# Block 1 of a retention and sliding-window encoder: weight chunks go ahead of raw pieces and stores in SyncE's queue, and one low part moves among the additions

## The chip, the cores and the metric

The kernel runs on one core of a Trainium2 chip. The metric is the device time of one execution in microseconds (us); lower is better. The kernel before takes 2468.24 us, the median of 3 runs (2468.12 to 2469.08).

## The reference

Two layers over x of 2048 tokens by 1024 channels, all float32:

```
h = x
h = h + retention(rmsnorm(h)) # q, k, v, gate = h @ w_in (1024 x 6144); 4 heads, chunkwise recurrence,
                              # o normalised per head, y = o * silu(gate), y @ w_out (2048 x 1024)
kb, vb = banded keys and values of rmsnorm(h) @ w_kv
h = h + swa(rmsnorm(h))       # q, gate = h @ w_in (1024 x 2048); window of 128 tokens with sinks,
                              # y = o * silu(gate), y @ w_out
return rmsnorm(h)
```

## The kernel before

**Blocks, heads and chunks.** The tokens are worked in 4 blocks of 512, each all the way through both layers. A block has four retention heads and then a "post" part with the second layer. The weights of a head come in 8 chunks, c0 to c7 (q, k, v in two halves, gate in two halves, output in two halves); the post part has 14. Each float32 operand is split into a high and a low part that TensorE can multiply, and each product is three matmuls (`three`, L674 to L676: high by high, high by low, low by high). A chunk is then 2048 KB of high and low parts. It needs 48 matmuls of 128x512 in every part of a head spoken of here. There are two chunk buffers, `whl0` and `whl1`, for even and odd chunks.

**Where the split chunks come from.** Block 0 loads raw weights, splits them (GpSimd the high part, VectorE the low part), uses them, and stores them to `split_w` in HBM (`store_chunk`, L419). Block 1 loads them from there (`load_split`, L438, in heads; L536 in the post part). `load_split` of chunk c waits on `w_used` until chunk c-2, which lay in the same buffer, has been used by TensorE. TensorE in its turn waits for a chunk's landing on `w_ready` (`w_wait`).

**The combining work of block 1.** Blocks 2 and 3 use other weights, sums of quarters of the raw ones. Block 1 makes these on the side, in each head six pieces, j = 0 to 5:

1. SyncE loads raw weights into `raw`, buffer j % 2, in two DMAs of 512 KB (`load_piece`, L463).
2. GpSimd forms the four sums (L619) and then the high part into `stage`, a part of `ff` (L625). There is one stage only, so the high part of piece j waits until both stores of piece j-1 have landed (`comb_stored`).
3. VectorE forms the low part of each piece but the fifth (`comb_less_hi`, L1857); of that one GpSimd does it itself. VectorE works in program order, so an instruction behind L1857 waits while L1857 waits for GpSimd's high part.
4. SyncE stores both parts in two DMAs of 1024 KB (`store_piece`, L473), after waiting for the low part.

The low parts of pieces 0, 1, 2, 3 stand at fixed places in VectorE's program: piece 0 between the two rotations (after q's low part, before the rotation of k, L1869), piece 1 behind k's low part, piece 2 just before the low parts of v (L1560), piece 3 behind the last state update, piece 5 behind the eight additions to the residual (L1978). TensorE starts the state updates and outputs of a head when its chunk c3 (second half of v) is done and two of the four low parts of v are there (`v_lo`).

**SyncE's queue.** SyncE issues all of these DMAs, in the order in which `combining_head` is written, and waits in that order. In a head h > 0 the order is: c0, c1, store of piece 5 of the head before, raw piece 1, c2, store 0, raw 2, c3, store 1, raw 3, c4, store 2, raw 4, c5, store 3, raw 5, c6, c7, store 4, raw piece 0 of the next head. In head 0 the raw pieces 0 and 1 stand first, behind a wait for the landing of all stores of block 0 (L433). ScalarE issues four stores of the finished rows of block 0 (L1276, 512 KB each) in head 0 of block 1.

Of the kernel before, what the change touches and what calls it, by code (L numbers as in the profile page):

```python
# [54 lines left out]
CHUNK = 2048  # L55
# [7 lines left out]
BLOCK_CHUNKS = HEADS * HEAD_CHUNKS + POST_CHUNKS  # L63
# [45 lines left out]
def build(nc, x, x_t, stream, rope_a, rope_b, mask, ident, ret_cols, gains, sinks, fnorm, out):  # L109
    with ExitStack() as ctx:  # L110
# [3 lines left out]
        def count(name, **kw):  # L114
            return Count(ctx.enter_context(nc.semaphore(name)), **kw)
# [118 lines left out]
        w_stored = [count(f"w_stored{i}", head=4, post=7, unit=16) for i in range(2)]  # L234
# [169 lines left out]
        def _(sp):  # L404
# [11 lines left out]
            def store_chunk(n):  # L416

                sp.wait_ge(w_ready[n % 2].sem, 16 * (n // 2 + 1))
                sp.dma_start(split_w[n * P:(n + 1) * P, :, 0:width(n)],  # L419
                             whl[n % 2][:, :, 0:width(n)].bitcast(F32)).then_inc(w_stored[n % 2].sem, 16)  # L420
# [8 lines left out]
                if n >= 1:  # L429
                    store_chunk(n - 1)  # L430
            store_chunk(BLOCK_CHUNKS - 1)
            for i in range(2):
                sp.wait_ge(w_stored[i].sem, 16 * (BLOCK_CHUNKS // 2))  # L433

            def load_split(at, c, src, width):

                sp.wait_ge(w_used.sem, at(w_used, c - 1))
                sp.dma_start(whl[c % 2][:, :, 0:width].bitcast(F32), src).then_inc(w_ready[c % 2].sem, 16)  # L438

            def split_rows(h, c):  # L440
                n = h * HEAD_CHUNKS + c
                return split_w[n * P:(n + 1) * P, :, :]
# [4 lines left out]
            def combining_head(b, h, last_store=None):  # L447
                at = Place("head", b, h)

                def load_piece(h, j):  # L450

                    if j >= 2:
                        sp.wait_ge(comb_lo.sem, Place("head", b, h)(comb_lo, j - 1))
                    elif h > 0:
                        sp.wait_ge(comb_lo.sem, Place("head", b, h - 1)(comb_lo, PIECES - 1 + j))
                    for i in range(2):
                        if j < 2:
                            n = h * HEAD_CHUNKS + 6 + i
                            src = stream[n * P:(n + 1) * P, :].rearrange("p (a i n) -> p a i n", a=2, i=2)[:, :, j, :]
                        else:  # L460
                            n = h * HEAD_CHUNKS + 2 + 2 * i
                            src = stream[n * P:(n + 2) * P, (j - 2) * 512:(j - 1) * 512].rearrange("(c p) n -> p c n", p=P)
                        sp.dma_start(raw[j % 2][:, i * HALF:(i + 1) * HALF].rearrange("p (a n) -> p a n", a=2), src).then_inc(comb_raw[j % 2].sem, 16)  # L463

                def store_piece(j):

                    sp.wait_ge(comb_lo.sem, at(comb_lo, j + 1))
                    for i in range(2):
                        if j < 2:
                            dst = comb_w[4 * h * P:4 * (h + 1) * P, i, j * 512:(j + 1) * 512]  # L470
                        else:
                            dst = vg_w[4 * h * P:4 * (h + 1) * P, i, (j - 2) * 512:(j - 1) * 512]
                        sp.dma_start(dst.rearrange("(q p) n -> p q n", p=P),  # L473
                                     stage[:, i, :].rearrange("p (q n) -> p q n", q=4)).then_inc(comb_stored.sem, 16)

                if h == 0:
                    load_piece(0, 0)
                    load_piece(0, 1)
                for c in range(3):
                    load_split(at, c, split_rows(h, c), CHUNK)  # L480
                    if c == 1 and h > 0:
                        last_store()
                        load_piece(h, 1)
                store_piece(0)
                load_piece(h, 2)
                load_split(at, 3, split_rows(h, 3), CHUNK)
                store_piece(1)
                load_piece(h, 3)
                load_split(at, 4, split_rows(h, 4), CHUNK)
                store_piece(2)  # L490
                load_piece(h, 4)
                load_split(at, 5, split_rows(h, 5), CHUNK)
                store_piece(3)
                load_piece(h, 5)
                for c in (6, 7):
                    load_split(at, c, split_rows(h, c), CHUNK)
                store_piece(4)
                if h < HEADS - 1:
                    load_piece(h + 1, 0)
                return lambda: store_piece(5)  # L500
# [40 lines left out]
            last_store = None  # L541
            for h in range(HEADS):
                last_store = combining_head(1, h, last_store)
# [1009 lines left out]
        def _(dve):  # L1553
# [56 lines left out]
            at = Place("start")  # L1610
# [24 lines left out]
            def one_block(b, first, last, combine=False):  # L1635
# [214 lines left out]
                def one_head(h, seam=False):  # L1850
                    at = Place("head", b, h)
                    n0 = h * HEAD_CHUNKS if first else None

                    def comb_less_hi(j):

                        dve.wait_ge(comb_hi.sem, at(comb_hi, j + 1))
                        dve.tensor_tensor(stage[:, 1, :].bitcast(F32R), raw[j % 2], stage[:, 0, :], ALU.subtract).then_inc(comb_lo.sem, 1)  # L1857
# [114 lines left out]
                    def add_to_h(n, t):  # L1972
                        if t < 3:
                            dve.wait_ge(out_mm.sem, at(out_mm, 3 * n + t + 1))
                        else:
                            dve.wait_ge(w_used.sem, at(w_used, 7 + n))
                        cols = hres[:, t, n * 512:(n + 1) * 512]
                        dve.tensor_tensor(cols, cols, ps[:, 4 * n + t, :], ALU.add).then_inc(h_add.sem, 2)  # L1978
# [22 lines left out]
                        split_chunk(n0 + 8)  # L2001
                    for t in range(TT):
                        add_to_h(1, t)
                    if combine:
                        comb_less_hi(5)

                if first:
                    for h in range(HEADS):
                        one_head(h)
                elif b >= FAST:  # L2010
                    for h in range(HEADS):
                        fast_head(h)
                else:
                    one_head(0, True)
                    with dve.Fori(1, HEADS) as h:
                        one_head(h)
                n0 = HEADS * HEAD_CHUNKS

                at = Place("post", b)
# [286 lines left out]
```

## Time and profile before

| | |
|---|---|
| median of 3 runs | 2468.24 us |
| the profiled execution, its own time | 2471.62 us |
| span of its trace | 2469.8 us |
| granted TensorE clock, mean | 0.994 |
| TensorE busy | 2410.3 us, 98% |
| VectorE, ScalarE, GpSimd busy | 58%, 27%, 17% |
| heads of block 1, as times in the span | 642 to 1101 us |
| DMA share of the 16 engines in 1000 to 1050 us | 1.00, at 383 GB/s |
| chunk load L438, median from issue to landing | 11.8 us (7.9 to 19.0) |
| stores L473, median to landing | 7.6 us (4.2 to 14.7) |
| raw pieces L463, median to landing | 9.5 us (4.2 to 15.4) |

Times of rows are microseconds from the start of the span. TensorE is busy for nearly the whole span, so what counts is each stretch in which it waits, and the stretches at half of its clock that come after longer waits. In the heads of block 1 every other engine has idle time, and the DMA engines are near their limit.

### The profile page before, as it was taken

The page shows a single profiled execution, that of the slowest core. Times are in us where ns is not written, and L with a number is a line of the kernel's source. Part 1 is how long each engine was busy: PE and PEld are TensorE (multiplying, and loading weights), DVE is VectorE, ACT ScalarE, POOL GpSimd, SP SyncE. Part 2 cuts the span into 40 slices and gives each one's busy share as a digit, 9 for nine tenths or more (in the row PEclk, how much of TensorE's full clock was granted, in tenths as well). Part 3 has the DMA queues.
Part 4 walks back from the last instruction along what each step waited for, and adds up shares of the span by engine and source line. Part 5 has one row for each costly group of instructions (what it writes and reads, how often), then busy time and mean ns, then how long its engine had stood idle before and what let it go on. Part 6 is the DMA issues. An engine that isn't in the chain of part 4 may idle for free.

```text
span 2469.8 us, 28619 instructions
## 1 busy us (share of the span) xinstructions
PE 2410.3 (98%) x11264; PEld 1978.4 (80%) x11264; DVE 1431.9 (58%) x2010; ACT 666.7 (27%) x1450; POOL 414.3 (17%) x310
## 2 busy tenths in 40 slices
PE   7999999999989999999999999999999999999998
PEld 6888888877768787878888888888888887888886
DVE  6555655677545545553758564655567745657374
ACT  2212312235121211121442231223352212313143
POOL 2111111221244545430001000000001100001000
PEclk9999999999999999999999999999999999999999
DMA  8667565645698898975259878775447977787433
GB/s 349 269 230 289 208 255 228 232 183 210 247 351 329 316 350 306 358 253 189 101 207 324 275 251 290 246 258 211 149 163 234 334 263 272 255 277 251 171 103 145
DMA packets 126393, 613.25 MB, mean 248 GB/s; under 512 B 8544, under 2 KB 9312, under 8 KB 104288
## 3 DMA queue, kind: packets, MB, share of 16 engines
q1 hardware_dynamic: 117424, 575.94, 64.5%
q10 hardware_dynamic: 8880, 36.18, 3.9%
q8 instruction: 49, 0.80, 0.1%
q14 instruction: 40, 0.33, 0.0%
HBM read 459.00 MB, written 153.09 MB: 248 GB/s over the span
## 4 chain that ended last, share of the span: by engine, by line
PE 83%; DVE 9%; DMA 4%; issue 2%; ACT 1%; POOL 1%; SPq 1%; DVEq 0%; ACTq 0%; POOLq 0%
PE ps L674 26%; PE ps L676 26%; PE ps L675 26%; DMA whl<-split_w 2%; PE ps L1127 2%; DVE ff L1857 1%; DMA comb_w<-ff 1%; DVE ff L2077 1%; PE ps L1137 1%; DVE ff L1965 1%; DVE fr L1556 1%; PE ps L935 1%; PE ps L822 1%; ACT ff L1424 1%; DVE mx L2117 1%
## 5 line engine op out<-in xcount | busy, mean ns | idle before, releaser
L674 PE MATMUL ps<-whl,xhi 128*128 128x512 f32 (+1 forms) x1088 | 418.4, 385 | 11.3 <-DMA whl<-split_w 6.9
L676 PE MATMUL ps<-whl,xlo 128*128 128x512 f32 (+1 forms) x1088 | 412.8, 379 | 0.0
L675 PE MATMUL ps<-whl,xhi 128*128 128x512 f32 (+1 forms) x1088 | 411.6, 378 | 0.0
L674 PE MATMUL ps<-xhi,whl 128*128 128x512 f32 x768 | 305.4, 398 | 21.6 <-DVE xlo L1560 16.2
L676 PE MATMUL ps<-xhi,whl 128*128 128x512 f32 x768 | 301.4, 392 | 0.0
L675 PE MATMUL ps<-xlo,whl 128*128 128x512 f32 x768 | 300.9, 392 | 0.0
L674 PE MATMUL ps<-whl,fr 128*128 128x512 f32 x704 | 282.1, 401 | 2.4 <-DVE whl L1598 2.1
L676 PE MATMUL ps<-whl,fr 128*128 128x512 f32 x704 | 278.8, 396 | 0.0
L675 PE MATMUL ps<-whl,fr 128*128 128x512 f32 x704 | 278.4, 395 | 0.0
L674 PEld LDWEIGHTS ps<-whl,xhi 128*128 128x128 f32 x1088 | 205.7, 189 | 50.4 <-DMA whl<-split_w 7.4
L676 PEld LDWEIGHTS ps<-whl,xlo 128*128 128x128 f32 x1088 | 205.5, 189 | 38.9
L675 PEld LDWEIGHTS ps<-whl,xhi 128*128 128x128 f32 x1088 | 205.8, 189 | 36.4
L674 PEld LDWEIGHTS ps<-xhi,whl 128*128 128x128 f32 x768 | 145.5, 189 | 51.5 <-issue 17.8
L674 PE MATMUL ps<-fr 128*128 128x512 f32 (+1 forms) x464 | 169.6, 365 | 5.3 <-DVE fr L1560 4.6
L676 PEld LDWEIGHTS ps<-xhi,whl 128*128 128x128 f32 x768 | 145.3, 189 | 31.3
L675 PEld LDWEIGHTS ps<-xlo,whl 128*128 128x128 f32 x768 | 145.7, 190 | 29.3
L675 PE MATMUL ps<-fr 128*128 128x512 f32 (+1 forms) x464 | 167.6, 361 | 0.0
L676 PE MATMUL ps<-fr 128*128 128x512 f32 (+1 forms) x464 | 167.4, 361 | 0.0
L674 PEld LDWEIGHTS ps<-whl,fr 128*128 128x128 f32 x704 | 132.4, 188 | 34.8 <-DVE whl L1598 2.3
L676 PEld LDWEIGHTS ps<-whl,fr 128*128 128x128 f32 x704 | 132.4, 188 | 32.0
L675 PEld LDWEIGHTS ps<-whl,fr 128*128 128x128 f32 x704 | 132.5, 188 | 30.4
L619 POOL TENSOR_TENSOR raw<-raw 128x512 f32<-128x512 f32 x96 | 143.9, 1499 | 16.9 <-DMA raw<-in_stream 11.2
(199 smaller groups left out, 3703.3 us busy)
## 6 DMA issues: line engine op xcount, KB each, us to landing
whl<-split_w SPq DMA_DIRECT2D x68, 2048.0 KB, 8.6
whl<-split_w SPq DMA_DIRECT2D x110, 1024.0 KB, 6.8
split_w<-whl SPq DMA_DIRECT2D x44, 2048.0 KB, 7.2
whl<-vg_w SPq DMA_DIRECT2D x64, 1024.0 KB, 6.7
raw<-in_stream SPq DMA_DIRECT2D x44, 1024.0 KB, 9.4
vg_w<-ff SPq DMA_DIRECT2D x32, 1024.0 KB, 8.3
raw<-in_stream SPq DMA_DIRECT2D x50, 512.0 KB, 9.5
whl<-comb_w SPq DMA_DIRECT2D x24, 1024.0 KB, 6.4
```

The costliest lines, as they stand in the source:

```text
L619: pool.tensor_tensor(dst, plus, minus, ALU.subtract).then_inc(comb_sum.sem, 1)
L674: pe.matmul(dst, lhs[0], rhs[0], start=start, stop=False)
L675: pe.matmul(dst, lhs[0], rhs[1], start=False, stop=False)
L676: return pe.matmul(dst, lhs[1], rhs[0], start=False, stop=stop)
L822: tr = pe.transpose(ps[:, 4 + t, e * P:(e + 1) * P], on[:, t, e * P:(e + 1) * P], idt[:, :])
L935: tr = pe.transpose(ps[:, 4 + t, e * P:(e + 1) * P], on[:, t, e * P:(e + 1) * P], idt[:, :])
L1127: mm = pe.matmul(ps[:, 4 + s % 2, r * 256:(r + 1) * 256], qt[:, i, n, 2 * r:2 * r + 2, :].rearrange("p f c -> p (f c)"), kwin[:, :, n // 2 ...
L1137: tr = pe.transpose(ps[:, 6, j * P:(j + 1) * P], probs[:, s % 2, j, :], idt[:, :])
L1424: act.activation(on[:, t, :], ps[:, 4 + t, :], ACT.Identity, scale=oscale[:, t:t + 1], bias=obias[:, t:t + 1]).then_inc(o_norm.sem, 1)
L1556: return dve.tensor_tensor(dst, src, hi.bitcast(F32), ALU.subtract).then_inc(c.sem, 1)
L1857: dve.tensor_tensor(stage[:, 1, :].bitcast(F32R), raw[j % 2], stage[:, 0, :], ALU.subtract).then_inc(comb_lo.sem, 1)
L1965: dve.tensor_tensor(on[:, t, :], on[:, t, :], sg[:, t, :], ALU.mult).then_inc(y_done.sem, 1)
```

## The change

Block 1's part of SyncE's program is put in another order, and one VectorE instruction moves.

- The wait for all stores of block 0 goes. The first chunk waits only for the stores from its own buffer, and is issued ahead of raw pieces 0 and 1; the second chunk waits for the stores from the other buffer.
- In every head c3 is issued before store 0 (and before raw piece 2). c4 stays behind store 1 and goes ahead of raw piece 3; c5 and c6 likewise go ahead of raw pieces 4 and 5. c7 comes behind raw piece 5.
- The low part of piece 5 goes behind the sixth addition to the residual instead of the eighth.

```
-            for i in range(2):
-                sp.wait_ge(w_stored[i].sem, 16 * (BLOCK_CHUNKS // 2))
...
                 if h == 0:
+                    sp.wait_ge(w_stored[0].sem, 16 * (BLOCK_CHUNKS // 2))
+                load_split(at, 0, split_rows(h, 0), CHUNK)
+                if h == 0:
                     load_piece(0, 0)
                     load_piece(0, 1)
-                for c in range(3):
+                    sp.wait_ge(w_stored[1].sem, 16 * (BLOCK_CHUNKS // 2))
+                load_split(at, 1, split_rows(h, 1), CHUNK)
+                if h > 0:
+                    last_store()
+                    load_piece(h, 1)
+                for c in (2, 3):
                     load_split(at, c, split_rows(h, c), CHUNK)
-                    if c == 1 and h > 0:
-                        last_store()
-                        load_piece(h, 1)
                 store_piece(0)
                 load_piece(h, 2)
-                load_split(at, 3, split_rows(h, 3), CHUNK)
                 store_piece(1)
+                load_split(at, 4, split_rows(h, 4), CHUNK)
                 load_piece(h, 3)
-                load_split(at, 4, split_rows(h, 4), CHUNK)
...
                     for t in range(TT):
                         add_to_h(1, t)
-                    if combine:
-                        comb_less_hi(5)
+                        if combine and t == 1:
+                            comb_less_hi(5)
```

SyncE's queue at the start of block 1, before. `whl` is the chunk buffers, `raw` the raw pieces; the first row is block 0's last store.

```order
L419 DMA split_w<-whl 128x4096 [waits w_ready1]
L463 DMA raw<-in_stream 128x2x512 [waits w_stored1,w_stored0]
L463 DMA raw<-in_stream 128x2x512 x3
L438 DMA whl<-split_w 128x4096 [waits w_used] x3
L473 DMA comb_w<-ff 128x4x512 [waits comb_lo]
```

And now:

```order
L419 DMA split_w<-whl 128x4096 [waits w_ready1]
L436 DMA whl<-split_w 128x4096 [waits w_used,w_stored0]
L461 DMA raw<-in_stream 128x2x512 x4
L436 DMA whl<-split_w 128x4096 [waits w_used,w_stored1]
L436 DMA whl<-split_w 128x4096 [waits w_used] x2
L471 DMA comb_w<-ff 128x4x512 [waits comb_lo]
```

The first chunk has moved ahead of the four raw DMAs, and four chunks instead of three stand before the first store (line numbers are two lower in the changed file here).

SyncE's queue in a later head, before, from the store of piece 5 of the head before (`vg_w`), over the stores of pieces 0 and 1 (`comb_w`):

```order
L473 DMA vg_w<-ff 128x4x512
L463 DMA raw<-in_stream 128x2x512 [waits comb_lo]
L463 DMA raw<-in_stream 128x2x512
L438 DMA whl<-split_w 128x4096 [waits w_used]
L473 DMA comb_w<-ff 128x4x512 [waits comb_lo]
L473 DMA comb_w<-ff 128x4x512
L463 DMA raw<-in_stream 128x2x512 [waits comb_lo]
L463 DMA raw<-in_stream 128x2x512
L438 DMA whl<-split_w 128x4096 [waits w_used]
L473 DMA comb_w<-ff 128x4x512 [waits comb_lo]
```

And now:

```order
L471 DMA vg_w<-ff 128x4x512
L461 DMA raw<-in_stream 128x2x512 [waits comb_lo]
L461 DMA raw<-in_stream 128x2x512
L436 DMA whl<-split_w 128x4096 [waits w_used] x2
L471 DMA comb_w<-ff 128x4x512 [waits comb_lo]
L471 DMA comb_w<-ff 128x4x512
L461 DMA raw<-in_stream 128x2x512 [waits comb_lo]
L461 DMA raw<-in_stream 128x2x512
L471 DMA comb_w<-ff 128x4x512 [waits comb_lo]
```

Chunk c3, which stood behind the first pair of stores and the raw piece, now stands directly behind c2 and ahead of that pair.

VectorE's end of a head, before (`hres` is the residual, the first `ff` row the low part of piece 5):

```order
L1978 TENSOR_TENSOR hres<-hres,ps 128x512 x7
L1857 TENSOR_TENSOR ff<-raw,ff 128x2048
```

And now:

```order
L1980 TENSOR_TENSOR hres<-hres,ps 128x512 x5
L1859 TENSOR_TENSOR ff<-raw,ff 128x2048
L1980 TENSOR_TENSOR hres<-hres,ps 128x512 x2
```

The low part of piece 5 has moved ahead of the last two additions.

## Rows read from the trace of the kernel before

**Rows 1.** Waits of TensorE in 630:1110: in total, how many, the longest.
```profile
PE ps L674 <- DMA whl<-split_w: 10.8, 5, 4.3
```

**Rows 2.** Timeline of TensorE in block 1: start, duration, instruction, idle time before it.
```profile
641.49 0.40 PE L676 MATMUL ps<-whl,fr 128*128 128x512 f32 x1
645.88 0.80 PE L674 MATMUL ps<-xhi,whl 128*128 128x512 f32 x1 [4.00 <-DMA whl<-split_w]
...
689.49 0.79 PE L674 MATMUL ps<-whl,xhi 128*128 128x512 f32 x1 [4.28 <-DMA whl<-split_w]
...
706.66 0.77 PE L674 MATMUL ps<-fr 128*128 128x512 f32 x1 [4.38 <-DVE fr L1560]
...
807.18 0.50 PE L674 MATMUL ps<-whl,xhi 128*128 128x512 f32 x1 [0.96 <-DMA whl<-split_w]
...
818.32 0.47 PE L674 MATMUL ps<-fr 128*128 128x512 f32 x1
```

**Rows 3.** TensorE in three stretches: length, busy (matmuls), granted clock, DMA share, GB/s.
```profile
645.90:652.70 6.80, 6.80 (x17) 0.55 0.52 224
707.20:710.60 3.40, 3.40 (x10) 0.58 1.03 387
1026.00:1040.00 14.00, 13.21 (x53) 0.88 1.02 402
```

**Rows 4.** Timeline of SyncE's queue, start of block 1.
```profile
631.11 2.59 SPq L463 DMA_DIRECT2D raw<-in_stream  x4
633.74 8.50 SPq L438 DMA_DIRECT2D whl<-split_w  x2
```

**Rows 5.** Line L438 in 855.9:856.3: issue to landing of one chunk.
```profile
DMA to landing us min/median/max: 8.9/8.9/8.9
```

**Rows 6.** Timeline of SyncE's queue in head 1.
```profile
790.73 0.92 SPq L473 DMA_DIRECT2D comb_w<-ff  x2
...
794.18 1.32 SPq L438 DMA_DIRECT2D whl<-split_w  x1
803.56 0.92 SPq L473 DMA_DIRECT2D comb_w<-ff  x2
```

**Rows 7.** Timeline of VectorE in head 1.
```profile
787.32 3.38 DVE L1857 TENSOR_TENSOR ff<-raw,ff 128x2048 fp32r<-128x2048 f32 x1
791.76 1.23 DVE L1869 TENSOR_TENSOR ff<-ps,cosa 128x1024 f32<-128x1024 f32 x1 [1.06 <-PE ps L676]
...
814.56 2.29 DVE L1857 TENSOR_TENSOR ff<-raw,ff 128x2048 fp32r<-128x2048 f32 x1 [5.26 <-POOL ff L625]
816.77 2.06 DVE L1560 SCALAR_TENSOR_TENSOR fr<-ps,vcol,fr 128x512 fp32r<-128x512 f32 x3
```

**Rows 8.** Timeline of GpSimd in head 1: high parts of pieces 1 and 2.
```profile
798.77 2.44 POOL L625 TENSOR_SCALAR ff<-raw 128x2048 fp32r<-128x2048 f32 x1 [4.18 <-DMA comb_w<-ff]
...
812.62 1.90 POOL L625 TENSOR_SCALAR ff<-raw 128x2048 fp32r<-128x2048 f32 x1 [3.87 <-DMA comb_w<-ff]
```

**Rows 9.** Line L473 in 790.7:791.6, the pair of stores of piece 0.
```profile
DMA to landing us min/median/max: 4.2/5.8/7.5
```

**Rows 10.** Line L473 in 856.3:857.3, the pair of piece 4, issued 0.4 us behind a chunk.
```profile
L473 SPq DMA_DIRECT2D vg_w<-ff x2: 433/470/508, 856.4 to 856.8; - x2
...
DMA to landing us min/median/max: 11.1/12.3/13.4
```

**Rows 11.** VectorE and ScalarE's queue in head 0, timelines.
```profile
671.04 2.29 DVE L1857 TENSOR_TENSOR ff<-raw,ff 128x2048 fp32r<-128x2048 f32 x1
...
687.50 1.67 ACTq L1276 DMA_DIRECT2D out<-hres  x2
```

**Rows 12.** Line L473 in 685.6:686.5, the pair of piece 1 of head 0.
```profile
DMA to landing us min/median/max: 7.1/10.9/14.7
```

**Rows 13.** Timelines of VectorE and TensorE at the end of head 3.
```profile
1102.16 2.28 DVE L1857 TENSOR_TENSOR ff<-raw,ff 128x2048 fp32r<-128x2048 f32 x1
...
1107.43 0.36 PE L674 MATMUL ps<-whl,xhi 128*128 128x256 f32 x1 [2.49 <-DVE xlo L1556]
```

More of the change, by code:

```diff
@@ L476, in combining_head @@
                 if h == 0:
+                    sp.wait_ge(w_stored[0].sem, 16 * (BLOCK_CHUNKS // 2))
+                load_split(at, 0, split_rows(h, 0), CHUNK)
+                if h == 0:
                     load_piece(0, 0)
                     load_piece(0, 1)
-                for c in range(3):
+                    sp.wait_ge(w_stored[1].sem, 16 * (BLOCK_CHUNKS // 2))
[4 more added lines that the diff above has]
+                for c in (2, 3):
                     load_split(at, c, split_rows(h, c), CHUNK)
-                    if c == 1 and h > 0:
-                        last_store()
-                        load_piece(h, 1)
                 store_piece(0)
                 load_piece(h, 2)
-                load_split(at, 3, split_rows(h, 3), CHUNK)
                 store_piece(1)
+                load_split(at, 4, split_rows(h, 4), CHUNK)
                 load_piece(h, 3)
-                load_split(at, 4, split_rows(h, 4), CHUNK)
                 store_piece(2)
+                load_split(at, 5, split_rows(h, 5), CHUNK)
                 load_piece(h, 4)
-                load_split(at, 5, split_rows(h, 5), CHUNK)
                 store_piece(3)
+                load_split(at, 6, split_rows(h, 6), CHUNK)
                 load_piece(h, 5)
-                for c in (6, 7):
-                    load_split(at, c, split_rows(h, c), CHUNK)
+                load_split(at, 7, split_rows(h, 7), CHUNK)
                 store_piece(4)
```

## The prediction

> **What bounds the kernel now.** I read the page first: TensorE is busy for 98% of the span, so only its waits, and the half-clock stretches behind them, can be won or lost. The diff touches SyncE's program and one VectorE instruction, both in the heads of block 1, so I asked for TensorE's waits there. Five waits for a weight chunk take 10.8 us in all [rows 1]; the timeline shows them, and which are large [rows 2]. In head 0 TensorE waits 4.0 us for c0 (645.88) and 4.3 us for c3 (689.49); then 4.4 us for VectorE's low parts of v (706.66). Heads 1 to 3 are alike: only about 1 us for c3, as at 807.18. The clock rows show what a wait drags along: behind the first one the granted clock is 0.55 for 6.8 us, behind the third 0.58 for 3.4 us, and behind the 1 us wait of head 3 it is 0.88 over 14 us [rows 3]. Half of 6.8 and of 3.4 us is 3.4 and 1.7 us lost. The clock is otherwise full, the upper of its levels 1.2 and 2.4 GHz.
>
> Next the other side, what the moved stores release. In head 1 VectorE's low part of piece 0 runs 787.32 to 790.70 [rows 7]; the store pair goes out at 790.73 [rows 6] and has landed 7.5 us after its second issue, at 798.6 [rows 9]; GpSimd's high part of piece 1 starts at 798.77, 0.1 us later [rows 8]; its low part ends at 803.56, where the next pair is issued [rows 6]; this lands just before 812.62, when the high part of piece 2 starts [rows 8]; the low part follows at 814.56 and the low parts of v at 816.77, of which the second is done at 816.77 + 2 x 0.69 = 818.15 [rows 7]. TensorE starts the first state update at 818.32 [rows 2]. So the chain store, high, low, store, high, low, v ends within 0.2 us of the moment when TensorE comes for it: there is no slack. It shows as a wait for c3 only since that wait comes first.
>
> **Start of the block.** The first chunk stood behind four raw DMAs, whose issue alone took 2.6 us [rows 4], and landed at 645.88. Its buffer is free when TensorE begins the last chunk of block 0. A chunk's 48 matmuls take (818.32 - 807.18) = 11.1 us [rows 2], so that is near 630. Issued then, it lands 8.9 us later [rows 5], at 639, and TensorE goes on at 641.7 without a wait. The second chunk goes out at 641.9 as before [rows 4] and is needed at 652.9; it lands near 651. That takes away the wait of 4.2 us and some 3 us of half clock: everything up to c3 comes 7.1 us earlier.
>
> **c3 in head 0.** It goes out when c1 is done, 641.7 + 2 x 11.1 = 664, lands at 673, and TensorE wants it at 689.49 - 4.28 - 7.1 = 678.1. This wait is gone as well, and TensorE is through c3 at 689.3. What is late next: the low part of piece 0 starts at 671.04 - 7.1 = 663.9 [rows 11] and ends at 666.2, but its stores are now issued behind c3. The nearest row for that is a pair issued 0.4 us behind a chunk, which landed 11.1 and 13.4 us after its issues [rows 10], 14.3 us after the chunk's issue. That gives 678.4. Then high part 1.9, low part 2.3 and the next pair at 682.6. Alone a pair takes 7.9 us from its first issue [rows 9] (690.5); before, with ScalarE's four stores beside it and a chunk ahead of it, 14.7 us from its second [rows 12] (697.7). ScalarE's stores hang on the masked scores, which follow the low part of piece 1, so they are still beside it, but no chunk is in flight. I take 693.5, nearer to the first. High 1.9, low 2.3, two low parts of v 1.4: the state update starts at 699.2 instead of 706.66. Head 0 gains 7.5 us (bounds 3.3 and 10.5); its clock loss is 2.3 instead of 1.7 (below). Term: -6.9.
>
> **c3 in heads 1 to 3.** c1 ends at 791.7, where VectorE's rotation of k starts [rows 7]; c3 goes out then instead of at 794.18 and lands at 800.6, well before it is wanted at 806.2. The 0.96 us wait is gone, and TensorE is ready for the state update at 818.32 - 0.96 = 817.36. But the low part of piece 0 ended at 790.7, 1 us before c1. Its stores now wait for SyncE to get past c3's wait (792.2 instead of 790.73), and then stand behind 2048 KB in the queue: they land at 792.7 + 13.4 = 806.1 instead of 798.6. High part 1.9 (2.4 before, beside VectorE's work), low part 2.3, next pair at 810.4 instead of 803.56. That one gains 1.0: nothing stands ahead of it, 7.9 us against 8.9. So 818.3, high 820.3, low 822.6, two of v 824.0, and the state update at 824.1 instead of 818.32: +5.8 us per head, a wait of 6.7 us where there was one of 1. c4 and c5 are issued behind the stores of pieces 1 and 2, whose low parts are late, at 811 and 823; c4 lands near 823, c5 near 836, the first wanted after 825 and the second after 849, so they cost nothing; without that cover a late c4 would cost at most its landing behind the raw piece. Term: 3 x 5.8 = +17.4, bounds per head -0.1 (stores not held up) and +7.
>
> The trace's clearest row is against a rule of the Trainium skill. "DMA: Bandwidth & Descriptors", section "Anatomy of one DMA", gives a DMA's time as a constant of some 2.0 us plus bytes over 436 GB/s. By that rule, as an estimate, chunk and pair together (4.2 MB) would be down 11.6 us after the chunk's issue, where the trace has 14.3 [rows 10], and a lone pair after 6.8 us, where it has 7.9 [rows 9]; each of heads 1 to 3 would lose 2.0 us instead of 5.8, and the sum below would be +1.9.
>
> **Clock.** No row has a wait of 6.7 us at this place; those of 4 us cost 3.4 and 1.7 us, that of 1 us in head 3 1.7 and those in heads 1 and 2 nothing. I take 2.3 per long wait, nearest to the row at 707.20, where the same matmuls follow (bounds 0 and 3.4). Three new ones, less the one that head 3 had: 6.9 - 1.7 = +5.2.
>
> **Low part of piece 5.** At the end of head 3 it ran 1102.16 to 1104.44, between the last addition and the low parts of the residual for which TensorE waited 2.49 us (1107.43) [rows 13]. Two additions earlier it fills time in which VectorE waits for TensorE, and the wait goes: -2.4. If its high part were late there, the additions would be held up, at most 2.3 us per head. In heads 1 to 3 it brings nothing: its stores still stand behind c1.
>
> **Sum.** -6.9 + 17.4 + 5.2 - 2.4 = +13.3 us on the profiled execution's 2471.62, so 2484.9. That execution was 3.4 us above the median, and a like one of the changed kernel would be too: 2481.5 in the median. Own range of this case: 2474 to 2488.
>
> **Rivals.**
> - Stores pass the chunk (not slower). c3 is read from HBM, stores are written to it; if the pair behind c3 takes 7.5 us all the same, the chain in heads 1 to 3 ends 1.5 later by the issue and 1.5 earlier by the rest: -0.1 each, and head 3's clock loss of 1.7 goes. Head 0 gains 4.2 more. Sum -0.3 - 1.7 - 11.1 - 2.4 = -15.5, so 2452.7. It decides from the point where the pair lands within 8 us of its issue. Against it: the pair in rows 10, read with rows 5, lands only after the chunk has. 8%.
> - Partly so: the pair overlaps the chunk's end, and lands half of the 5.4 us between chunk and pair earlier. Each head then loses 3.1 us: 9.3 + 5.2 - 6.9 - 2.4 = +5.2, so 2473.4, or about no change with cheaper clock. The rule of the Trainium skill weighed above gives the +1.9 there, on this side too. 10%.
> - ScalarE's stores collide with the pair in head 0 as badly as before (697.7): 4.2 us less gain, 2485.7. 9%.
> - The change doesn't do what it says: c0's landing was not the last thing that TensorE waited for at 645.88. Then head 0 keeps 7 us, 2488. The row names the DMA, so 3%.
> - My forecast: 70%.
>
> The measurement can tell about 0.2%, 4.9 us. Faster by more: the first rival and a little, 9%. Within: most of the second, 9%. Slower: 82%. The range 2469 to 2489 leaves out the first rival and 4% above.
>
> **What would show it.** Right: no wait for the chunk loads L436 in TensorE's list; three new waits of some 6 to 7 us for VectorE's low parts of v, in heads 1 to 3, with half clock behind them; a first pair of stores per head that lands 13 us after its issue; head 0's state update near 699; the wait for the low parts of the residual gone. Wrong: that pair landing within 8 us, or TensorE's waits for v under 3 us.

## The result, and the profile after

The change makes the kernel slower: 2481.72 us in the median of 5 runs (2479.23 to 2482.02) against 2469.08 us (2468.12 to 2474.11) for the kernel before in the same session, a ratio of 1.0047 with a 95% interval of 1.0032 to 1.0061. The profiled execution took 2481.79 us, its span 2480.0 us.

TensorE's waits in the heads of block 1 of the changed kernel (line numbers of the code behind the diff have moved by two: L674 is L676 here, L1857 is L1859, L1560 is L1562):

```profile
PE ps L676 <- DVE fr L1562: 26.0, 4, 7.7
PE ps L824 <- DVE ff L1967: 3.9, 7, 0.7
PE ps L676 <- DVE ff L1872: 1.5, 1, 1.5
PE ps L676 <- DVE xlo L1558: 0.3, 1, 0.3
```

No wait for a chunk is left, where there were 10.8 us [rows 1]. In their place stand four waits for the low parts of v, 26.0 us, where there had been one of 4.4. TensorE's timeline, the rows that answer to [rows 2] and [rows 13], first the last matmul of block 0 and the first of block 1:

```profile
640.03 0.39 PE L678 MATMUL ps<-whl,fr 128*128 128x512 f32 x1
640.26 0.40 PE L676 MATMUL ps<-xhi,whl 128*128 128x512 f32 x1
...
669.14 0.50 PE L676 MATMUL ps<-whl,xhi 128*128 128x512 f32 x1 [1.47 <-DVE ff L1872]
...
694.35 0.77 PE L676 MATMUL ps<-fr 128*128 128x512 f32 x1 [5.02 <-DVE fr L1562]
...
812.72 0.77 PE L676 MATMUL ps<-fr 128*128 128x512 f32 x1 [6.69 <-DVE fr L1562]
...
930.22 0.77 PE L676 MATMUL ps<-fr 128*128 128x512 f32 x1 [6.65 <-DVE fr L1562]
...
1049.56 0.77 PE L676 MATMUL ps<-fr 128*128 128x512 f32 x1 [7.67 <-DVE fr L1562]
...
1117.74 0.36 PE L676 MATMUL ps<-whl,xhi 128*128 128x256 f32 x1 [0.28 <-DVE xlo L1558]
```

TensorE goes from block 0 into block 1 without a gap. In each head the wait stands at the first state update. Before, the same matmuls of heads 2 and 3 started without one:

```profile
928.18 0.45 PE L674 MATMUL ps<-fr 128*128 128x512 f32 x1
...
1039.67 0.39 PE L674 MATMUL ps<-fr 128*128 128x512 f32 x1
```

With these rows the four heads can be cut at their state updates, which takes out that block 0 was 1.5 us shorter in this execution (its last matmul is at 640.03 instead of 641.49):

| stretch | before | after | difference |
|---|---|---|---|
| block 0's last matmul to head 0's state update | 65.2 | 54.3 | -10.9 |
| to head 1's | 111.7 | 118.4 | +6.7 |
| to head 2's | 109.9 | 117.5 | +7.6 |
| to head 3's | 111.5 | 119.3 | +7.9 |
| to the first product of the post part | 67.8 | 68.2 | +0.4 |
| all of it | 465.9 | 477.7 | +11.8 |

(The last row's +0.4 is a gain of 2.2 us at its end, and half clock at its start.)

The queue in head 1, against [rows 6], and the landing of the two stores, against [rows 9]:

```profile
780.64 0.34 SPq L436 DMA_DIRECT2D whl<-split_w  x1
781.02 0.98 SPq L471 DMA_DIRECT2D comb_w<-ff  x2
782.05 4.56 SPq L461 DMA_DIRECT2D raw<-in_stream  x2
798.94 0.92 SPq L471 DMA_DIRECT2D comb_w<-ff  x2
```

```profile
DMA to landing us min/median/max: 10.9/12.0/13.0
```

c3 is issued, 0.4 us later the pair of stores, and the second store lands 13.0 us after its issue instead of 7.5. The chain behind it on GpSimd and VectorE, against [rows 8] and [rows 7]:

```profile
794.69 1.90 POOL L627 TENSOR_SCALAR ff<-raw 128x2048 fp32r<-128x2048 f32 x1 [11.21 <-DMA comb_w<-ff]
...
807.02 1.90 POOL L627 TENSOR_SCALAR ff<-raw 128x2048 fp32r<-128x2048 f32 x1 [2.33 <-DMA comb_w<-ff]
```

```profile
796.62 2.29 DVE L1859 TENSOR_TENSOR ff<-raw,ff 128x2048 fp32r<-128x2048 f32 x1 [8.29 <-POOL ff L627]
...
808.96 2.29 DVE L1859 TENSOR_TENSOR ff<-raw,ff 128x2048 fp32r<-128x2048 f32 x1 [6.78 <-POOL ff L627]
811.17 0.74 DVE L1562 SCALAR_TENSOR_TENSOR fr<-ps,vcol,fr 128x512 fp32r<-128x512 f32 x1
```

GpSimd waits 11.2 us for the store instead of 4.2; VectorE stands 6.8 us at the low part of piece 2 instead of 5.3, and reaches it later, and the low parts of v, which TensorE needs, are behind it. What the clock did behind each of the four waits:

```profile
694.00:704.00 10.00, 9.65 (x31) 0.69 1.00 396
812.00:822.00 10.00, 9.29 (x33) 0.79 1.03 398
930.00:940.00 10.00, 9.79 (x32) 0.72 1.04 407
1049.00:1062.00 13.00, 12.44 (x43) 0.77 1.01 393
```

One minus the granted clock, times the stretch, is 3.1, 2.1, 2.8 and 3.0 us lost.

### The profile page after: what moved, and what is told of

The parts are those of the page before. It is cut to its first block, busy times and chain, and to the rows that moved or that the text cites. A ratio compares the mean times of both kernels' runs of the same rounds, so it can differ in the third digit from the quotient of the medians.

```text
span 2480.0 us, 28620 instructions
## 1 busy us (share of the span) xinstructions
PE 2410.5 (97%) x11264; PEld 1978.6 (80%) x11264; DVE 1433.9 (58%) x2010; ACT 665.6 (27%) x1450; POOL 418.9 (17%) x310
## 4 chain that ended last, share of the span: by engine, by line
PE 83%; DVE 8%; DMA 4%; issue 2%; ACT 1%; POOL 1%; SPq 0%; DVEq 0%; POOLq 0%; ACTq 0%
PE ps L676 26%; PE ps L678 26%; PE ps L677 26%; DMA comb_w<-ff 3%; PE ps L1129 2%; DVE ff L1859 1%; DVE ff L2079 1%; PE ps L1139 1%; DVE ff L1967 1%; PE ps L937 1%; POOL ff L627 1%; DVE fr L1562 1%; DVE fr L1558 1%; PE ps L824 1%; ACT ff L1426 1%
## 5 line engine op out<-in xcount | busy, mean ns | idle before, releaser
L676 PE MATMUL ps<-whl,xhi 128*128 128x512 f32 (+1 forms) x1088 | 417.2, 383 | 3.7 <-DVE xlo L1558 2.2
L676 PE MATMUL ps<-xhi,whl 128*128 128x512 f32 x768 | 304.1, 396 | 17.6 <-DVE xlo L1562 16.1
L676 PE MATMUL ps<-whl,fr 128*128 128x512 f32 x704 | 281.1, 399 | 2.3 <-DVE whl L1600 2.1
L676 PEld LDWEIGHTS ps<-whl,xhi 128*128 128x128 f32 x1088 | 204.9, 188 | 42.7 <-issue 3.9
L676 PE MATMUL ps<-fr 128*128 128x512 f32 (+1 forms) x464 | 173.2, 373 | 27.1 <-DVE fr L1562 26.2
L676 PEld LDWEIGHTS ps<-xhi,whl 128*128 128x128 f32 x768 | 144.8, 189 | 46.5 <-issue 17.7
L677 PE MATMUL ps<-fr 128*128 128x512 f32 (+1 forms) x464 | 170.6, 368 | 0.0
L678 PE MATMUL ps<-fr 128*128 128x512 f32 (+1 forms) x464 | 170.3, 367 | 0.0
L676 PEld LDWEIGHTS ps<-whl,fr 128*128 128x128 f32 x704 | 132.2, 188 | 34.8 <-DVE whl L1600 2.3
L621 POOL TENSOR_TENSOR raw<-raw 128x512 f32<-128x512 f32 x96 | 150.8, 1571 | 43.5 <-DMA raw<-in_stream 37.8
## 6 DMA issues: line engine op xcount, KB each, us to landing
raw<-in_stream SPq DMA_DIRECT2D x50, 512.0 KB, 13.3
```

Source lines behind the costliest of these rows:

```text
L621: pool.tensor_tensor(dst, plus, minus, ALU.subtract).then_inc(comb_sum.sem, 1)
L676: pe.matmul(dst, lhs[0], rhs[0], start=start, stop=False)
L677: pe.matmul(dst, lhs[0], rhs[1], start=False, stop=False)
L678: return pe.matmul(dst, lhs[1], rhs[0], start=False, stop=stop)
```

## The experiments

All ratios are to the kernel before in the same session, with 95% intervals. A gain or loss in us beside a ratio is worked out from the ratio; the medians can differ from it by a microsecond or two. Waits are TensorE's in the heads of block 1.

**The start alone.** The kernel before, with c0 ahead of the raw pieces and the waits for the stores split by buffer:

```
-            for i in range(2):
-                sp.wait_ge(w_stored[i].sem, 16 * (BLOCK_CHUNKS // 2))
...
+                    sp.wait_ge(w_stored[0].sem, 16 * (BLOCK_CHUNKS // 2))
+                load_split(at, 0, split_rows(h, 0), CHUNK)
```

> The kernel before with the start of the block alone changed: c0 ahead of raw pieces 0 and 1 and behind its own buffer's stores only. My theory (the three parts are independent, and this one is a gain): TensorE's 4.0 us wait for c0 and the half clock behind it go, and the order behind it is the old one; about 7 us faster, 2462 us, with the waits of 4.3 us for c3 and some 4 us for the low parts of v in head 0 still there. Rival (the next wait in head 0 swallows it, since the combining chain there starts from GpSimd's inverse root and the raw pieces, not from TensorE): those two waits grow by 4 to 7 us, and the time is that of before within 2 us.

Measured: 0.9978 (0.9969 to 0.9987), 5.4 us faster (4.4 by the medians). The wait for c0 is gone, those for c3 (4.8) and v (4.3) in head 0 are there, and one of 1.5 us is new. My theory stands; the gain is somewhat under 7.

**c3 alone.**

```
-                store_piece(0)
-                load_piece(h, 2)
                 load_split(at, 3, split_rows(h, 3), CHUNK)
+                store_piece(0)
+                load_piece(h, 2)
                 store_piece(1)
```

> The kernel before with c3 alone moved, ahead of store 0 and raw piece 2 in every head. My theory (the stores stand behind the chunk, and the chain through GpSimd's stage ends with VectorE's low parts of v): heads 1 to 3 each lose 6 to 8 us at the first state update, head 0 gains some 2 us; 2486 to 2490 us, and TensorE waits 6 to 7 us for the low parts of v in each of heads 1 to 3. Rival (the loss comes from the other moves, c4 to c6 ahead of the raw pieces, or from the start of the block shifting everything): within 3 us of before.

Measured: 1.0108 (1.0092 to 1.0123), 27 us slower (25 by the medians), well above what I expected.

```profile
PE ps L674 <- DVE fr L1560: 26.8, 4, 7.4
PE ps L674 <- DMA whl<-split_w: 6.6, 3, 4.0
PE ps L822 <- DVE ff L1965: 3.8, 7, 0.7
```

The four waits for v are there with no other part of the change present: the rival is out. Cut at the state updates as in the table above, head 0's comes 4.4 us earlier than before (60.8 us behind block 0's last matmul instead of 65.2), and the four stretches behind it are 7.7, 7.7, 6.9 and 2.9 us longer: 20.8 us in all. The 2486 to 2490 us that I expected are 14 to 18 above the kernel before as timed beside this run (2472.19). Head 0 then waits 1.6 us for c4, which is in the first of them. The rest of the excess is not in this trace: the profiled execution took 2492.72 us, 4.6 less than the median of 2497.33, and the other three had a mean granted clock of 0.989 to 0.990 where it had 0.992. Why they did stays open.

**The low part of piece 5 alone.**

```
                         add_to_h(1, t)
-                    if combine:
-                        comb_less_hi(5)
+                        if combine and t == 1:
+                            comb_less_hi(5)
```

> The kernel before with only the low part of piece 5 moved ahead of the last two additions. My theory: the wait of 2.5 us for the residual's low parts at the end of head 3 goes, nothing else moves; 2.4 us faster, 2466.5 us. Rival (the additions behind it are held up by a late high part of piece 5 in each head): 0 to 7 us slower.

Measured: 0.9990 (0.9981 to 0.9999), 2.5 us faster, with an interval of 0.2 to 4.7 us; the wait at the end of head 3 falls from 2.5 to 0.3 us. As expected.

**c4 to c6 alone, ahead of raw pieces 3 to 5.**

```
-                load_piece(h, 3)
                 load_split(at, 4, split_rows(h, 4), CHUNK)
+                load_piece(h, 3)
```

(and the same for c5 with piece 4 and c6 with piece 5)

> The kernel before with only c4, c5 and c6 each ahead of the raw piece 3, 4 and 5 that stood before it. My theory: nothing waits for these chunks or pieces, so within 2 us of before, and no new waits of TensorE. Rival (the raw pieces behind the chunk make the high parts late and with them the low parts of piece 3 or 4): 2 to 6 us slower.

Measured: 1.0004 (0.9995 to 1.0013), and no new wait above 1 us. This part does nothing by itself, to within 3 us.

**Start and c3 together.** The kernel before, with both of these edits and no other:

```
-            for i in range(2):
-                sp.wait_ge(w_stored[i].sem, 16 * (BLOCK_CHUNKS // 2))
...
+                    sp.wait_ge(w_stored[0].sem, 16 * (BLOCK_CHUNKS // 2))
+                load_split(at, 0, split_rows(h, 0), CHUNK)
...
                 load_split(at, 2, split_rows(h, 2), CHUNK)
+                load_split(at, 3, split_rows(h, 3), CHUNK)
                 store_piece(0)
                 load_piece(h, 2)
-                load_split(at, 3, split_rows(h, 3), CHUNK)
```

> The kernel before with the start of the block and c3's move together, c4 to c6 and piece 5 as before. It tells where the parts fail to add up: c3's move alone cost 1.0108, start and piece 5 together bring 0.9968, and the whole change costs 1.0047. Theory one (the start and c3's move help each other in head 0: only with both is TensorE early and the chunk there): 1.006 to 1.008, and head 0's waits are those of the changed kernel, 6.5 us in all. Theory two (c4 to c6 ahead of the raw pieces is what softens c3's move): 1.009 or more.

Measured: 1.0058 (1.0044 to 1.0072). Theory two is out. Theory one gives the place: head 0's waits are 1.5, 5.0 and 1.7 us, 8.2 in all, where they were 12.7 before, 10.5 with the start alone and 13.0 with c3's move alone, so 10.9 if the two simply added. The 1.7 us are for c4, and the changed kernel doesn't have them. In size the help is small. From block 0's last matmul to the first product of the post part the start alone is 3.2 us shorter than before, c3's move alone 20.8 longer, and both together 15.1 longer, 2.6 less than the sum. The product of the two ratios would be 1.0086, 7 us above what was measured, but the intervals of the three runs leave this anywhere from 1 to some 13 us (my estimate), and 4.6 us of it lie between the median and the profiled execution of the run of c3 alone. With piece 5 (0.9990) the 1.0058 gives 1.0048; the whole change measured 1.0047. The parts add up.

**c3 from ScalarE's queue.** The changed kernel, with c3 taken out of SyncE's program and put into ScalarE's, where it stands between the high parts of q and k (ScalarE's loop over heads 1 to 3 is also written out):

```
+                    if b == 1:
+                        n = h * HEAD_CHUNKS + 3
+                        act.wait_ge(w_used.sem, at(w_used, 2))
+                        act.dma_start(whl[1][:, :, :].bitcast(F32),
+                                      split_w[n * P:(n + 1) * P, :, :]).then_inc(w_ready[1].sem, 16)
```

> The changed kernel, but c3 of each head of block 1 is issued from ScalarE's queue, at the same moment (when c1 is used), so that store 0 is neither behind c3's wait nor behind its bytes in SyncE's queue. Theory one (order within one queue holds the stores back): the pair of piece 0 lands 8 to 10 us after its issue, the waits for the low parts of v in heads 1 to 3 shrink to under 3 us; 2452 to 2462 us. Theory two (the 16 DMA engines are simply full, whichever queue the bytes are in): the pair still takes 12 us or more, the waits stay at 4 us or more, and the time stays above 2470 us.

Measured: 1.0026 (1.0014 to 1.0037). SyncE now issues the pair first, ScalarE the chunk 0.7 us later; the landing of the pair in head 1:

```profile
DMA to landing us min/median/max: 4.6/9.3/14.1
```

The first store is quick, but the second takes 14.1 us, as if it stood behind the chunk, and TensorE waits 5.8, 5.9, 4.9 and 5.1 us for v. The chunk is late too: it lands after 12.9 us, where it took 8.6 in the changed kernel. Theory two: another queue doesn't protect the stores. Both are drawn out, as they would be if they shared the DMA engines, which the windows above show at a share of 1.00 to 1.04.

**c3 between store 0 and raw piece 2**, in the changed kernel, all in SyncE's queue:

```
-                for c in (2, 3):
-                    load_split(at, c, split_rows(h, c), CHUNK)
+                load_split(at, 2, split_rows(h, 2), CHUNK)
                 store_piece(0)
+                load_split(at, 3, split_rows(h, 3), CHUNK)
                 load_piece(h, 2)
```

> The changed kernel with c3 between store 0 and raw piece 2. My theory (within SyncE's queue bytes go in the order of issue, so the pair of stores, issued 1 us before the chunk, is not held up by it, and the chunk is ahead of the raw pieces): the pair lands after 7.5 us, c3 before it is wanted in heads 1 to 3, no wait for v over 1 us there; head 0 as in the changed kernel; 12 to 15 us faster than before, ratio 0.994 to 0.995. Rival (all that matters is that chunk and stores share the 16 DMA engines in these microseconds, in whichever order, as when c3 came from ScalarE's queue): the pair takes over 12 us here too, and heads 1 to 3 wait over 4 us; ratio above 1.002.

Measured: 0.9979 (0.9970 to 0.9988). Landing of the pair in head 1, and the waits:

```profile
DMA to landing us min/median/max: 4.2/5.8/7.5
```

```profile
PE ps L676 <- DVE fr L1562: 10.6, 4, 7.0
PE ps L824 <- DVE ff L1967: 4.0, 8, 0.7
PE ps L676 <- DMA whl<-split_w: 3.0, 4, 1.7
```

The chunk is issued 1.0 us behind the first store here, 0.7 us in the run before; the second store takes 7.5 us here and 14.1 there. The landings within the one queue came in the order of issue: the pair, then the chunk (11.9 us after its issue), then the raw piece. With two queues the chunk, issued last, landed 0.9 us ahead of the second store. The rival is out, though one head waits more for v than the 1 us that I allowed (1.9 us in head 3). The time missed my 0.994, for head 0: the wait for v there is 7.0 us, not 5.0, since the pair of piece 1 took 14.5 us:

```profile
DMA to landing us min/median/max: 9.0/11.7/14.5
```

The same pair in the changed kernel:

```profile
DMA to landing us min/median/max: 4.2/6.3/8.5
```

ScalarE's four stores are not the whole reason, since in both kernels the first of them is issued 1.8 us behind the pair. What differs is the transfer ahead of it. In the changed kernel raw piece 2 had landed when the pair was issued (679.6); here, behind c3, it landed 4 us after (684.1). With the raw piece still ahead but ScalarE's stores moved away, in the run of the spread stores below, the pair took 9.6 us. So it is the two together that make it 14.5.

**c3 put back.** The changed kernel with c3 behind store 0 and raw piece 2:

```
-                for c in (2, 3):
-                    load_split(at, c, split_rows(h, c), CHUNK)
+                load_split(at, 2, split_rows(h, 2), CHUNK)
                 store_piece(0)
                 load_piece(h, 2)
+                load_split(at, 3, split_rows(h, 3), CHUNK)
                 store_piece(1)
```

> The changed kernel with c3 put back behind store 0 and raw piece 2, in all heads. My theory (the moved c3 is the whole loss, the rest a gain): the waits of 6.7 us for the low parts of v in heads 1 to 3 go, c3's waits come back (4.8 us in head 0, about 1 us after it), and the time is that of the start and the low part of piece 5 together, 0.9978 x 0.999, 0.997 of before or 7 to 8 us faster. Rival (c4 to c6 ahead of the raw pieces carry a loss of their own): not faster than before.

Measured: 0.9964 (0.9950 to 0.9977), 2462.80 us, against 2472.98 for the kernel before in that session.

```profile
PE ps L676 <- DMA whl<-split_w: 8.5, 6, 4.5
PE ps L824 <- DVE ff L1967: 4.2, 8, 0.7
PE ps L676 <- DVE fr L1562: 3.7, 2, 3.6
```

The waits for v in heads 1 to 3 are gone, c3's are back. One line of the change turns a gain of 0.36% into a loss of 0.47%.

**The low part of piece 2 behind the low parts of v**, in the changed kernel:

```
-                    if combine:
-                        comb_less_hi(2)
                     for t in range(TT):
                         dve.wait_ge(v_hi.sem, at(v_hi, t + 1))
                         scaled_less_hi(vhl[1][:, t, :], ...)
+                    if combine:
+                        comb_less_hi(2)
```

> The changed kernel, with VectorE's low part of piece 2 behind the low parts of v instead of ahead of them. My theory (TensorE's 6.7 us is paid only since VectorE stands in program order at the low part of piece 2): the waits for the low parts of v go in all four heads, though the stores still land late; the first state update on VectorE is late instead, and TensorE waits 1 to 3 us for the second one; ratio to before 0.995 to 0.999. Rival (the stage chain limits the head as such): the wait turns up in full, 5 us or more, one step on, and the time stays above 1.003.

Measured: 0.9970 (0.9961 to 0.9979). The stores still land late, and yet the loss is gone: no wait for v is left. What VectorE's order cost is shown; the place that I named for the rest was wrong. It is mainly c4, and not the second state update:

```profile
PE ps L676 <- DMA whl<-split_w: 11.3, 7, 3.7
PE ps L824 <- DVE ff L1967: 5.0, 7, 1.8
```

c4 stands in SyncE's queue behind store 1, which waits for the late low part of piece 1; TensorE now comes for it 3.7, 1.6, 2.0 and 1.9 us early.

**Both steps.** The changed kernel with c3 between store 0 and raw piece 2, and the low part of piece 2 behind those of v:

```
                 store_piece(0)
+                load_split(at, 3, split_rows(h, 3), CHUNK)
                 load_piece(h, 2)
...
-                    if combine:
-                        comb_less_hi(2)
                     for t in range(TT):
...
+                    if combine:
+                        comb_less_hi(2)
```

> Both: c3 between store 0 and raw piece 2, and the low part of piece 2 behind the low parts of v. My theory: in heads 1 to 3 TensorE waits for nothing at this place; in head 0 the wait for v is replaced by 2 to 3 us for the second state update; ratio to before 0.990 to 0.993, the fastest of all. Rival (c3 between is enough, the low part's place only matters when it is late): the same as c3 between alone within 2 us.

Measured: 0.9962 (0.9948 to 0.9975), 2462.43 us. Faster than c3 between alone by more than 2 us, but short of 0.993: in head 0 the wait for v turned into one of the same size for c4, behind the same pair of stores, which took 14.7 us here, and beside ScalarE's four. In heads 1 and 2 a wait of 1.4 us before the second state update is left, where I had expected none.

```profile
700.76 0.79 PE L676 MATMUL ps<-whl,xhi 128*128 128x512 f32 x1 [5.01 <-DMA whl<-split_w]
```

**ScalarE's stores spread.** The kernel with both steps, with the four stores of head 0 issued one, one and two ahead of the high parts of the second, third and fourth state:

```
-                    if seam:
-                        store_out(b - 1)
...
                     for c in range(1, TT):
+                        if seam:
+                            store_out(b - 1, ((0,), (1,), (2, 3))[c - 1])
                         act.wait_ge(a_new.sem, at(a_new, c))
```

> c3 between store 0 and raw piece 2, the low part of piece 2 behind those of v, and ScalarE's four stores of finished rows spread behind its work on v and on the state in head 0, so that they don't share the engines with the stores of piece 1 and c4. My theory: the wait of 5.0 us for c4 in head 0 and its half clock go: 4 to 7 us faster than the same kernel without the last step, ratio to before 0.993 to 0.995. Rival (the same bytes only collide later, or ScalarE's issues hold up the high parts of the state): no faster than 0.996.

Measured: 0.9962 (0.9948 to 0.9976). The wait for c4 in head 0 is gone, and another has come:

```profile
727.75 0.66 PE L824 MATMUL ps<-idt,ff 128*128 128x128 f32 x4 [3.29 <-DVE ff L1967]
```

The rows of x for block 1 go where the finished rows of block 0 lay, so they are loaded only when the four stores have landed, and VectorE waits for them before it gates y. The rival's first half is what happened.

**The low part of piece 2 one state update later.** The kernel of the spread stores (best_b in the expectation), with this edit in VectorE's program:

```
-                    if combine:
-                        comb_less_hi(2)
...
                     state_update(0)
                     state_lo(1)
+                    if combine:
+                        comb_less_hi(2)
                     statistics(0)
```

> As best_b, but the low part of piece 2 stands one step further on, behind the first state update and its low part. My theory: the wait of 1.4 us before the second state update in heads 1 and 2 goes as well: 1 to 3 us faster than best_b. Rival (a later low part makes store 2 and with it raw pieces 4 and 5 late): the same or slower.

Measured: 1.0013 (1.0004 to 1.0022), slower than the spread stores alone by more than 10 us, nearly all in head 0:

```profile
734.35 3.64 DVE L1967 TENSOR_TENSOR ff<-ff 128x512 f32<-128x512 f32 x2 [16.05 <-DMA hres<-in_x]
```

x was issued 2.6 us later than with the spread stores alone, landed after 16.2 us instead of 11.5, and TensorE waited 13.8 us at its transposes. In heads 1 to 3 the wait of 1.4 us did not go: it is 1.7 to 1.8, one state update further on. My expectation failed in both halves. That a later store 2 pushed x back is argued from their order in the trace, not shown by a run of its own.

Of the kernels that beat both of the given ones, the fastest three can't be told apart: c3 put back (0.9964), both steps (0.9962) and the spread stores (0.9962). The low part of piece 2 moved alone (0.9970) isn't clear of them either. The first is the simplest.

## Why the prediction was right

The forecast was 2481.5 us; 2481.72 was measured. By its own steps:

- **Start of the block.** c0's wait gone, no wait for c1 either. Right. VectorE's rotation of q, which follows c0, starts 11.4 us behind block 0's last matmul instead of 18.6, so the 7.1 us are there at this point. Alone the start is worth 5.4 us in the end.
- **c3 in head 0.** No wait for c3. The state update was to start at 699.2, which is 57.7 us behind block 0's last matmul; it started 54.3 behind it. So the gain was 3.4 us larger than forecast, and two landings were mis-sized. The pair of piece 0 was taken to land 14.3 us after c3's issue, by a row in which the pair stands 0.4 us behind the chunk; here it was issued 4.6 us behind, at the end of the low part, and landed 12.9 us after c3's issue. The pair of piece 1 was taken to need 10.9 us from its first issue, and needed 8.9; nothing was in flight ahead of it here. The rival in which ScalarE's stores collide with it as badly as before is out by this landing.
- **c3 in heads 1 to 3.** The pair behind the chunk took 13.0 us, 13.4 forecast; TensorE waited 6.7, 6.7 and 7.7 us, 6.7 forecast; the pair took 13.2 and 14.2 us in heads 2 and 3, which is the extra microsecond of head 3. The rival in which the stores pass the chunk is out by these rows; the one in which they overlap its end would have had a wait of 4. c3 alone, c3 put back and the low part of piece 2 moved show the three links of the step: the move causes it, undoing it removes it, and VectorE's order carries it to TensorE.
- **The rule of the Trainium skill.** The section that the prediction weighs in "DMA: Bandwidth & Descriptors" gives its fit for DMAs that GpSimd issues; these are SyncE's. Chunk and pair were down 13.9 us after the chunk's issue (780.64 to 794.5), where the estimate by that fit was 11.6.
- **Clock.** 2.3 us per long wait were taken; 2.1, 2.8 and 3.0 were lost at the state updates of heads 1 to 3, and 3.1 at head 0's. The price of a wait isn't fixed: behind c0's wait of some 4 us the clock was 0.55 over 6.8 us before [rows 3], and 0.75 over as long in the runs of c3 alone and of the low part of piece 5 alone. One minus the clock, times the stretch, gives 3.1 and 1.4 us for the first two of rows 3, where the prediction wrote 3.4 and 1.7.
- **Low part of piece 5.** 2.2 us of the 2.4 in the trace; the run of its own (0.9990) agrees within its interval.
- **Sum.** +13.3 forecast, +11.8 by the table above: head 0 gained 3.4 us more, the stretches behind it lost 1.8 more. That the median lies 0.2 us from the forecast is luck. The profiled execution was forecast at 2484.9 and took 2481.79, 3.1 us less: 1.5 of this is the sum, and 1.5 is block 0, which was shorter. The forecast then took off 3.4 us, on the ground that the profiled execution would again lie above the median; it lay at it (2481.79 against 2481.72). The two errors cancel. The mechanism is the one foreseen; its terms are right to 3.4 us in head 0 and to 1.8 behind it.
- **c4 to c6** were costed at nothing, and are nothing within 3 us (1.0004).

**A wait not foreseen.** TensorE waits 1.5 us for the rotated products of k (669.14). VectorE is 2 us late with them, since two instructions of the rotation of q before them take 1.7 us each instead of 0.7. They now run while GpSimd forms its sums (650.96 to 656.7); before, GpSimd was done at 657.7 and the rotation began at 660.05. That the sums are what slows them is not tested by a run. The first two rows are from before, the others from after:

```profile
662.44 0.69 DVE L1872 TENSOR_TENSOR ff<-ff 128x512 f32<-128x512 f32 x1
663.05 0.69 DVE L1873 TENSOR_TENSOR ff<-ff 128x512 f32<-128x512 f32 x1
...
653.85 1.69 DVE L1874 TENSOR_TENSOR ff<-ff 128x512 f32<-128x512 f32 x1
655.45 1.77 DVE L1875 TENSOR_TENSOR ff<-ff 128x512 f32<-128x512 f32 x1
```

The wait itself costs little, since TensorE waits 5.0 us for v behind it all the same.

The trace of before held nearly the whole answer in one row, the landing of the stores of piece 4 behind c7 [rows 10]; the rest was to notice that the chain through the one stage ended 0.2 us before TensorE came for it.

## What to carry to other kernels

A short wait of the bounding engine for a transfer can hide a second chain that ends at the same moment; before moving the transfer ahead of another one in its queue, follow what the other one releases, and take its new landing from a row where it already stands behind such a transfer. If something small must overtake something large, put it ahead in the same queue: here another queue didn't do it. Work that is not urgent should not stand in an in-order engine's program ahead of work that the bounding engine needs next. But its own successors set how far back it may go: the low part of piece 2 gained behind the low parts of v, and one state update further on, where its store and the load of x were late, it cost over 10 us.

## What was unexpected

- A store issued 0.3 us before a chunk on another queue took 14.1 us to land; one issued 0.6 us before it on the same queue took 7.5 us.
- The same pair of stores beside the same four stores of ScalarE took 8.5 us with nothing ahead of it, and 14.5 with one raw piece still in flight ahead.
- Two instructions of VectorE took 1.7 us instead of 0.7 when an earlier start put them beside GpSimd's sums.
- The three fastest kernels lose their time in different places of head 0 (c3, c4, the load of x), and come out equal.
